# Latent attention: unscaled exponentials to the transposes, inverse sums spread by matmuls and multiplied into the output of a pair of heads

## The reference

```python
q_nope, q_rope = q[..., :QK_NOPE], q[..., QK_NOPE:]
q_lat = jnp.einsum('bshn,chn->bshc', q_nope, w_uk) * ATTN_SCALE
...
s = (jnp.einsum('bqhc,bkc->bhqk', ql, c_kv)
     + jnp.einsum('bqhr,bkr->bhqk', qr, k_rope))
p = jax.nn.softmax(s.astype(jnp.float32), axis=-1).astype(c_kv.dtype)
return jnp.einsum('bhqk,bkc->bqhc', p, c_kv)
...
o = jnp.einsum('bshc,chv->bshv', o_lat, w_uv)
return o.reshape(B, S, N_HEADS * V_HEAD) @ w_o
```

## Time and profile before

| | before |
|---|---|
| median of 3 runs | 3321.98 us (3320.85 to 3323.76) |
| profiled execution | 3322.28 us |
| its span | 3320.6 us |
| PE / PEld / DVE / ACT / POOL busy | 94% / 77% / 51% / 35% / 18% |
| the 64 blocks of the attention | 1363.4 us to 1535.8 us of the span |

### The profile page before, as it was taken

The page is one execution under the profiler, slowest core; times in us unless marked ns, Lnnn a source line. Parts: engine busy times, 40 slices in busy tenths (PEclk is TensorE's granted clock), DMA queues, the critical chain, the costliest instruction groups (busy, mean ns, idle before and its releaser), DMA issues.

```text
span 3320.6 us, 40657 instructions
## 1 busy us (share of the span) xinstructions
PE 3125.5 (94%) x14594; PEld 2540.3 (77%) x14594; DVE 1684.9 (51%) x2717; ACT 1167.3 (35%) x2037; POOL 600.4 (18%) x353
## 2 busy tenths in 40 slices
PE   5999989999999999788999999997999999869999
PEld 5888888888888888576888887765777778657777
DVE  4554566545564345885411141764665415646663
ACT  2222232222232323564322223534443325343442
POOL 0100000000000000102344434023112330241113
PEclk9999978999999999899999999897999997989999
DMA  5555522555544232101232323012111220121112
GB/s 194 195 174 175 170 70 84 184 186 166 165 134 133 92 105 79 42 12 48 83 97 92 102 89 99 10 58 89 45 39 41 87 83 20 45 95 40 44 39 83
DMA packets 88027, 314.12 MB, mean 95 GB/s; under 512 B 10192, under 2 KB 10960, under 8 KB 87760
## 3 DMA queue, kind: packets, MB, share of 16 engines
q1 hardware_dynamic: 64992, 233.65, 21.7%
q0 software_dynamic: 19488, 71.31, 6.3%
q10 hardware_dynamic: 3408, 7.25, 0.7%
HBM read 307.98 MB, written 2.10 MB: 93 GB/s over the span
## 4 chain that ended last, share of the span: by engine, by line
PE 60%; issue 25%; DVE 7%; POOL 6%; DMA 1%; ACT 1%; ACTq 0%; POOLq 0%; SPq 0%; DVEq 0%
PE psum L378 49%; POOL w_lo L359 6%; PE psum L2102 4%; PE psum L1073 2%; PE psum L467 2%; PE psum L723 1%; PE psum L1042 1%; DVE small L1119 1%; DVE pt_lo L1138 1%; DVE tb L529 1%; DMA ada_first<-ada_in 1%; DVE h_lo L538 1%; DVE ada_acc L709 1%; DVE ta L672 1%; PE psum L2046 1%
## 5 line engine op out<-in xcount | busy, mean ns | idle before, releaser
L359 POOL TENSOR_TENSOR w_lo<-raw,w_hi 128x1024 fp32r<-128x1024 f32 x219 | 530.9, 2432 | 1752.8 <-ACT w_hi L333 1570.7
L378 PE MATMUL psum<-h_hi,w_hi 128*128 128x512 f32 x1824 | 495.6, 398 | 20.9 <-DVE h_lo L538 11.6
L378 PE MATMUL psum<-h_lo,w_hi 128*128 128x512 f32 x1824 | 485.8, 392 | 0.0
L378 PE MATMUL psum<-h_hi,w_lo 128*128 128x512 f32 x1824 | 485.7, 392 | 0.0
L378 PEld LDWEIGHTS psum<-h_hi,w_hi 128*128 128x128 f32 x1824 | 342.9, 189 | 109.4 <-DVE h_lo L538 17.8
L378 PEld LDWEIGHTS psum<-h_lo,w_hi 128*128 128x128 f32 x1824 | 343.5, 188 | 75.6
L378 PEld LDWEIGHTS psum<-h_hi,w_lo 128*128 128x128 f32 x1824 | 343.6, 188 | 74.0
L347 ACT ACTIVATE w_hi<-raw 128x1024 fp32r<-128x1024 f32 x256 | 257.8, 1048 | 155.5 <-DMA raw<-stream_in 155.5
L353 DVE TENSOR_TENSOR w_lo<-raw,w_hi 128x1024 fp32r<-128x1024 f32 x192 | 227.9, 1222 | 107.2 <-ACT w_hi L347 100.6
L333 ACT ACTIVATE w_hi<-raw 128x1024 fp32r<-128x1024 f32 x177 | 184.6, 1051 | 214.8 <-DMA raw<-stream_in 107.7
L849 ACT ACTIVATE a_hi<-tb 128x512 f32 (+1 forms) x88 | 55.6, 632 | 542.6 <-DVE tb L894 542.6
(11 more groups left out here) (408 smaller groups left out, 4901.5 us busy)
## 6 DMA issues: line engine op xcount, KB each, us to landing
raw<-stream_in SPq DMA_DIRECT2D x433, 512.0 KB, 3.5
ada_raw<-ada_in POOLq DMA_DIRECT2D x128, 512.0 KB, 4.6
ada_first<-ada_in POOLq DMA_DIRECT2D x2, 2048.0 KB, 20.7
ada_first<-ada_in SPq DMA_DIRECT2D x2, 2048.0 KB, 26.0
X<-xT_in ACTq DMA_DIRECT2D x1, 2048.0 KB, 9.7
out_x<-X SPq DMA_DIRECT2D x8, 256.0 KB, 2.5
qt_hi<-qr_hi ACTq DMA_DIRECT2D x16, 64.0 KB, 2.0
qt_lo<-qr_lo ACTq DMA_DIRECT2D x16, 64.0 KB, 2.1
```

Source lines behind the costliest of these rows:

```text
L359: pool.tensor_tensor(w_lo[:, u % RING], raw[:, u % RAW], w_hi[:, u % RING].bitcast(F32), ALU.subtract).then_inc(lo_ready, 1)
L378: mm = pe.matmul(dst, w[wi], m[mi], start=(first and n == 0), stop=(last and n == total - 1), skip_group_check=skip)
```

## The change

In the latent attention scale(k) goes. T(k) takes the unscaled exponentials and waits for E(k). E(k) writes its sums to `stat`. Once per pair DVE inverts eight columns of sums (`invert_sums`, behind lo in step 0 of the next pair). PE spreads them over a bank (`spread_sums`, in step 1 between S and T; eight fp32 matmuls, each with one column of sums repeated 64 times as weights and the identity as the moving side). ACT copies the bank to `rstd` (`take_sums`, step 2). DVE multiplies the pair's output by it into `std` (`low`, kind "pv", step 2). ACT makes `on_hi` from `std` in step 3 instead of step 2, and DVE `on_lo` in step 3 (kind "o"). Behind the last block all of this stands in one chain. The spread is a fifth group on the four banks.

```diff
             def turn(k):
-                pe.wait_ge(probs_scaled.sem, probs_scaled.at((L, k)))
+                if A["gate"] is None:
+                    pe.wait_ge(probs.sem, probs.at((L, k)))
+                else:
+                    pe.wait_ge(probs_scaled.sem, probs_scaled.at((L, k)))
...
                 maximum(k + 1)
-                scale(k)
+                if A["gate"] is not None:
+                    scale(k)
...
+            def spread_sums(pe, p):
+                g = own[L, "events"]["r", p]
+                free_bank(pe, g)
+                pe.wait_ge(inverses.sem, inverses.at((L, "r", p)))
+                for side in range(2):
+                    for i in range(4):
+                        mm = pe.matmul(bank(g)[64 * side:64 * side + 64, i * P:(i + 1) * P],
+                                       head_sum(2 * p + side, i).broadcast_to((P, 64)), ident[:],
+                                       start=(i == 0), stop=(i == 3), skip_group_check=True)
+                spread.give(mm, (L, "r", p))
+            def invert_sums(dve, p):
+                dve.wait_ge(probs.sem, probs.at((L, 8 * p + 7)))
+                row = 1 + 2 * (p % 2)
+                inverses.give(dve.reciprocal(stat[:, row:row + 2], stat[:, row:row + 2]), (L, "r", p))
+            def take_sums(act, p):
+                act.wait_ge(spread.sem, spread.at((L, "r", p)))
...
+                evac_hi.give(act.activation(rstd[:], bank(g), ACT.Copy), g)
...
                 elif kind == "pv":
-                    evac_split_act(act, g, on_hi[:, p])
+                    act.wait_ge(evac.sem, evac.at(("g", g)))
+                    part_hi.give(act.activation(on_hi[:, p], std[:], ACT.Copy), (L, "o", p))
...
                 if kind == "pv":
-                    evac_split_dve(dve, g, on_hi[:, p], on_lo[:, p])
+                    dve.wait_ge(prod.sem, prod.at(("g", g)))
+                    dve.wait_ge(evac_hi.sem, evac_hi.at(own[L, "events"]["r", p]))
+                    evac.give(dve.memset(small[:, 0, 0:1], 0.0), ("g", own[L, "events"]["r", p]))
+                    evac.give(dve.tensor_tensor(std[:], bank(g), rstd[:], ALU.mult), ("g", g))
                     return
+                if kind == "o":
+                    split_value_dve(dve, (L, "o", p), std[:], on_hi[:, p], on_lo[:, p])
...
                 elif k == 4 * HEADS:
-                    if who != "pe":
+                    if who == "pe":
+                        spread_sums(eng, 7)
+                    elif who == "act":
+                        take_sums(eng, 7)
                         todo = [("pv", 7)]
+                    else:
+                        invert_sums(eng, 7)
+                        todo = [("pv", 7), ("o", 7)]
```

More of the change, by code:

```diff
@@ L1016, in plan_softmax @@
             for k in range(4 * A["tasks"]):
-                for signal in (scores, peak, probs, probs_scaled, turned, turned_hi, turned_lo):
+                for signal in (scores, peak, probs, turned, turned_hi, turned_lo):
                     signal.plan((L, k))
+                if A["gated"]:
+                    probs_scaled.plan((L, k))
         def softmax_pe(pe, L, A, extra):
@@ L1098, in softmax_act @@
                     act.wait_ge(turned.sem, turned.at((L, k - 2)))
+                if A["gate"] is None and i == 0 and t >= 4:
+                    act.wait_ge(spread.sem, spread.at((L, "r", t // 2 - 2)))
                 probs.give(act.activation(A["p"][:, k % 2, 0:w], psum[:, 4 + k % 2, 0:w], ACT.Exp,
                                           bias=small[:, 1, k % 4:k % 4 + 1],
-                                          accum_out=small[:, 2, k % 4:k % 4 + 1]), (L, k))
+                                          accum_out=A["total"](t, i)), (L, k))
                 extra(act, "act", k, 0)
@@ L1258, in plan_mla, with plan_heads @@
             own[L, "unit_of"] = unit_of
+            def plan_heads(p):
+                for signal in (inverses, spread):
+                    signal.plan((L, "r", p))
+                for signal in (part_hi, h_ready):
+                    signal.plan((L, "o", p))
+                evac_hi.plan(events["r", p])
+                evac.plan(("g", events["r", p]), ("g", events["pv", p]))
             for kind in "qkv":
@@ L1263, in plan_mla @@
                 p = t // 2
+                if i == 1 and t >= 2 and t % 2 == 0:
+                    group("r", p - 1)
                 if i == 2 and t >= 2 and t % 2 == 0:
-                    evac_hi.plan(events["pv", p - 1])
-                    evac.plan(("g", events["pv", p - 1]))
+                    plan_heads(p - 1)
                 kind = {(0, 0): "q", (0, 2): "k", (1, 0): "v"}.get((t % 2, i))
@@ L1274, in plan_mla @@
             prod.plan(("pv", L, HEADS - 1))
[L1275 to L1276 removed]
+            group("r", 7)
+            plan_heads(7)
             for p in range(8):
@@ L1294, in mla_scores, with head_sum @@
                                 [(kt_hi[:, t % 4], kt_lo[:, t % 4])], skip=True)
+        def head_sum(t, i):
+            row = 1 + t % 4
+            return stat[:, row, i:i + 1]
         def mla_free(pe, g, t):
@@ L1301, in kernel_program @@
             "tasks": HEADS, "width": lambda t, i: S, "scores": mla_scores,
-            "gate": lambda t, i: None, "p": ta, "slots": 2,
+            "gate": None, "total": lambda t, i: head_sum(t, i), "p": ta, "slots": 2,
             "place": lambda m, t, rows, n, i: (pt2_hi, pt2_lo)[m][0:rows, t % 2, 0:n, i * P:(i + 1) * P],
@@ L1395, in run @@
                     if who == "pe":
+                        if phase == 0 and at_ == (0, 1) and p >= 1:
+                            spread_sums(eng, p - 1)
                         kind = {(0, 0): "q", (0, 2): "k", (1, 0): "v"}.get(at_)
@@ L1450, in mla_pe @@
             u, g = own[L, "wo"], own[L, "wog"]
-            pe.wait_ge(evac.sem, evac.at(("g", own[L, "events"]["pv", 7])))
+            pe.wait_ge(h_ready.sem, h_ready.at((L, "o", 7)))
             for n in range(NC):
```

22 lines of the change are left out of this document (16 added, 6 removed).

## The result

| | before | after |
|---|---|---|
| median of 19 runs each | 3321.62 us | 3332.82 us |
| lowest to highest | 3314.74 to 3333.06 | 3324.33 to 3337.48 |
| ratio, 95% interval | | 1.0029 (1.0019 to 1.0039) |
| profiled execution / its span | 3322.28 / 3320.6 us | 3329.22 / 3327.5 us |

The change made the kernel slower by 0.29%, 9.6 us by the ratio and 11.2 by the medians. The forecast was 3332.5 us. Single runs of one kernel lie up to 18 us apart, so what follows is read from the traces, inside the attention.

The account below looks back on a forecast made before the run. PE's list (18.2 us of work in a 21.18 us pair) and its waits for E bound it. Pairs 1 to 6 +8.0, pair 0 -1.0, pair 7 +0.25, end +3.4: +10.6 on 3322.28, less 0.3, 3332.5 us; range 3318 to 3341.

Parts of the forecast that it names:

- rival 1: Attention: DVE alone was the bound, so 30 us go and 3.4 come back at the end, 3296 us; chance 0.05.
- Rival 2: Attention: PE becomes the bound and every stall goes, waits for E included; -5.7 us, 3316.5 us; chance 0.14.
- S4 to S6: PE between score products 4 and 6 of a pair: `on_hi` delays E4, which S6 awaits; 0.65 us lost.
- S6 to S7: PE between score products 6 and 7: T4 no longer waits for scale, E5 just hidden; 0.75 us gained.
- S7 to S0': PE from score product 7 to the next pair's first: 4.05 us of work in 4.64; 0.6 us gained.
- S0' to S3': PE between the next pair's score products 0 and 3: E0' wait unchanged, then all PE work; gain 0.
- `on_hi` between hi(2) and E4: ACT in S4 to S6: `on_hi`, 0.63 us, now stands ahead of E4; 4.17 us become 4.8.
- The spread: PE, S3' to S4': hides behind nothing, +2.03 us (1.87 records, 0.16 width changes); first start to T 1.9 to 2.1.
- rival 3: The spread's two halves overlap: 0.94 us instead of 1.87, eight times, 3325 us; chance 0.12.
- Pair 0: First pair of the attention, without spread or `on_hi`: between -0.7 and -1.4 us, taken as -1.0.
- Pair 7: Last pair, without q, k, v: +1.1 us up to S4 and -0.85 after it, together +0.25.
- the end: Behind the last V: spread, copy, product, then `on_hi` in one chain put Wo 3.4 us later.

Follow-up runs that it names:

- e1: The kernel before with scale(k) left out and nothing put in its place; ratio to before 0.9973.
- e3: The changed kernel with `on_hi` and `on_lo` moved from step 3 to step 5; ratio to before 1.0019.
- e2: The changed kernel with every spread issued twice; ratio to before 1.0033.
- e4: The changed kernel with the last pair's inverse and spread put ahead of the last output product V; ratio to before 1.003.
- e11: The changed kernel run once more, unchanged; ratio to before 1.0035.
- e5: The changed kernel with a full-width spread, 4 matmuls of 128 weights, DVE writing 512 reciprocals into `rstd` instead of 8; ratio to before 1.0058.
- e6: The changed kernel with the spread's eight matmuls alternating between upper and lower 64 output rows; ratio to before 1.0023.
- e8: The kernel before, scaling kept, with only the split of k moved to step 5 and that of v to step 6; ratio to before 0.9973.
- e9: The changed kernel with full-width spread from 8 reciprocals and a copy, k, v and output splits in steps 5, 6, 4, last spread early; ratio to before 0.9977.
- e10: The kernel of e8 with the split of the output also moved, from step 2 to step 4; ratio to before 0.9971.

## Why the prediction was right

**The bound.** Shown: PE's list and the waits for E decide, not DVE's time. Without scaling (e1) the attention loses 9.9 of the 37.8 us of DVE's time; rival 1 is out. Rival 2, every stall gone, is out by the table: S0' to S2' is 2.64 us in after as before.

**The segments.** Period forecast 22.5 us, measured 21.98. Segment by segment, forecast and measured in after: S4 to S6 +0.65 and +0.53; S6 to S7 -0.75 and -0.71; S7 to S0' -0.6 and -0.68; S0' to S3' 0 and 0. The step "`on_hi` between hi(2) and E4" is shown by e3, which takes exactly that back. It was 0.12 too dear, since I took the duration, 0.63, for the time it holds ACT, 0.52.

**The spread.** That it hides behind nothing is shown by e2, where twice the records lengthen only this segment. The size was off, 2.03 us forecast and 1.67 measured, and one sign failed with it: from the first start to T it is 1.51 us, not 1.9 to 2.1. The price of a record was nearly right, 0.109 us for 0.117, 1.75 for 1.87 in sum. The changes of form cost 0.35 for 0.16. What I had at nothing is the overlap of the two halves at the seam, -0.43: I had named it under rival 3 ("only the seam could overlap"), and gave it no term. The overlap and the changes of form are errors of opposite sign and partly hid each other.

**Pairs 0 and 7, the end.** Pair 0 -0.5 for -1.0; here the clock matters, since by windows of 2 us PE runs at 1.2 GHz for the first 5 us of the attention in before and 6 in after (3 to 4 in e4 and e11, where pair 0 gives -1.3). Pair 7 -0.2 for +0.25, the end +3.0 for +3.4. The chain behind V is shown by e4.

**What stood in no step.** The sum with the measured sizes is 6 x 0.83 - 0.5 - 0.2 + 3.0 = 7.3 us. Two clock falls added 3.2 in this profile (three 4.8 in e11's), and the first unit of Wo ran 1.0 us shorter in after. So the forecast of +10.6 is near the measured 9.6 partly by luck: the spread, forecast too dear by 0.36 eight times, stood for clock falls that I had not seen coming. Where the falls come from is not settled. They were in all five profiles with `on_hi` ahead of E4 and a spread once per pair (after, e4, e5, e6, e11), 2 or 3 pairs each, 11 in all, and each began 1.3 to 2.0 us behind the S6 that had waited 1.6 us for E4. They were in none of the other eight, one execution each, which include e2 with the same stall of 1.6 us and more PE work in the pair. So the stall goes with them and is not enough; that it brings them was not tried by itself.

**A version that beats both.** e8, e9 and e10 are each 0.2 to 0.3% faster than before, with intervals that overlap. In e8 what wins is moving the splits of k and v to later steps; that they stood early has nothing to do with the change, it was so before. With them moved, the unscaled form (e9) and the scaling (e8) cost the same within what the runs tell; but e9 is not the change as it was made, it also has the full-width spread, the output split in step 4 and the early last spread. The order of the change with only k and v moved was not run.

## What to carry to other kernels

An engine that stands for another can win no more than its own idle time: here PE's 3.0 us per pair, and the relief put 1.7 us of new work on the very engine that was to gain. Before taking work off a busy engine, write down one period of the waiting one, and ask of each stall which chain ends second. Here PE stood at T3 for the scaling; without the scaling it stood just as long at S6, one row further, for E4. Once that was seen, moving two splits to later steps (e8, -0.27%) was worth more than taking 128 instructions off DVE (after, +0.29%).

## What the runs showed of the hardware

- Records of a 128-column fp32 matmul followed one another every 0.109 us with 64 weights (after) and every 0.11 with 128 (e9): half the weights did not make a record shorter. Entering and leaving the 64-weight form cost 0.35 us per spread; the full-width spread of e9, 8 records in 0.89 us, had none of it. The Trainium skill, page "TensorEngine Tiling (Array Packing)", section Key Properties, says that a change of tiling mode drains the engine; the trace agrees in kind, with 0.10 us of pause at each of the two changes.
- The same section of the Trainium skill says that different tiles can work in parallel. The trace agrees, and the order of issue decides how much: with the four matmuls of each half together the second half starts 0.49 us behind the first, and the 16 records take 1.51 us; where the halves alternate they take 1.03 (e6).
- DVE's reciprocal took 0.19 us for 8 columns (e9) and 3.34 for 512 (e5), 6.5 ns a column, where a product of 512 takes 0.69 and a copy of the same repeated columns 0.43 (e9).
- PE's granted clock fell to 1.2 GHz for about 3.4 us in periods of 23.5 us in which PE never stood longer than the 1.6 us for E4, and came back while PE was working without a pause (4.00 of the 4.00 us from 1492.00).
